# Two bidirectional mixers of a diffusion backbone: projections of the next group and head beside this one's work

## The reference, cut to what matters

```python
xbc = silu(short_conv(h @ w_in[x, B, C]) + conv_b)              # 3 taps; per group: 4 x tiles, B, C
lmat = exp(where(tril, acs[:, None] - acs[None, :], -inf))      # acs: cumulative dt * a, per head
y = (C B^T * lmat) @ (x dt) + (C @ state) * exp(acs)            # per chunk, forward and backward
state = state * exp(acs[-1]) + B^T @ (x dt exp(acs[-1] - acs))  # from chunk to chunk
out = rmsnorm((y_f + y_b + x * skip) * silu(z)) @ w_out         # SSD: 4 groups of 8 heads

q, k, v = silu(short_conv(h @ w_in)); q = l2norm(q) * dk ** -0.5; k = l2norm(k)
m = strict_tril((k beta) @ k^T * decay); tmat = inverse(I + m)  # 128 x 128 per chunk
v_new = tmat @ (v beta - (k beta exp(gc)) @ s)                  # chunk after chunk
o = (q exp(gc)) @ s + tril(q @ k^T * decay) @ v_new
s = s * exp(gc[-1]) + (k exp(gc[-1] - gc))^T @ v_new
out = (rmsnorm(o_f + o_b) * silu(z)) @ w_out                    # GDN: 8 heads, dk 128, dv 256
```

## Time and profile before

| | us |
|---|---|
| median of three runs (lowest, highest) | 6237.69 (6228.37, 6243.76) |
| the profiled execution: its own time, its span | 6234.22, 6232.4 |
| TensorE busy over the span | 4920.7 (79%) |
| VectorE busy | 4364.5 (70%) |
| ScalarE busy | 1670.4 (27%) |
| GpSimd busy | 1605.7 (26%) |

### The profile page before, as it was taken

How to read it: one execution, slowest core, us unless ns; L and a number is a source line. 1 busy time by engine, 2 the same in 40 slices (tenths; PEclk the granted TensorE clock), 3 DMA queues, 4 the chain that set the end, 5 groups by cost and what they waited for, 6 DMA issues and landing times. The chain is left out here.

```text
span 6232.4 us, 77006 instructions
## 1 busy us (share of the span) xinstructions
PE 4920.7 (79%) x27154; PEld 4314.5 (69%) x27154; DVE 4364.5 (70%) x7749; ACT 1670.4 (27%) x2016; POOL 1605.7 (26%) x1060
## 2 busy tenths in 40 slices
PE   6677676854689999997777777777854589999997
PEld 2566665754469888996766666666844359988896
DVE  1555554379759999998455555565279759999997
ACT  0122222211343333332212211121211243333332
POOL 0000000011026667773000000000011016666774
PEclk7788888877569999998888988899977559999999
DMA  8100110110159999995000000000110159999996
GB/s 359 40 28 21 38 38 4 54 38 23 71 234 402 401 401 397 397 398 209 29 25 25 25 25 21 16 18 21 54 38 23 54 217 401 401 402 398 397 395 261
DMA packets 340323, 1059.27 MB, mean 170 GB/s; under 512 B 28272, under 2 KB 135024, under 8 KB 316656
## 3 DMA queue, kind: packets, MB, share of 16 engines
q1 hardware_dynamic: 192624, 519.24, 22.0%
q0 software_dynamic: 147456, 536.94, 21.9%
HBM read 998.92 MB, written 57.15 MB: 169 GB/s over the span
## 5 line engine op out<-in xcount | busy, mean ns | idle before, releaser
L1836 POOL DMA_INDIRECT dense_ring<-in_peer_u_rows,dense_eid x512 | 723.3, 1413 | 934.6 <-DVEq L1952 583.8
L1608 POOL TENSOR_TENSOR top_w_lo<-top_w,top_w_hi 128x1024 fp32r<-128x1024 f32 x32 | 96.1, 3021 | 3342.4 <-ACTq L1576 3342.4
L1836 POOL DMA_INDIRECT dense_ring<-in_peer_v_rows,dense_eid x512 | 786.1, 1535 | 290.6 <-DVE dense_acc L1993 189.0
L1850 PE MATMUL psum<-peer_in_hi,dense_u_hi 128*128 128x384 f32 x2048 | 690.1, 337 | 44.8 <-DVE dense_u_lo L1958 44.8
L1850 PE MATMUL psum<-peer_in_hi,dense_u_lo 128*128 128x384 f32 x2048 | 690.4, 337 | 0.0
L1850 PE MATMUL psum<-peer_in_lo,dense_u_hi 128*128 128x384 f32 x2048 | 688.8, 336 | 0.0
L1993 DVE SCALAR_TENSOR_TENSOR dense_acc<-dense_ring,dense_weight,dense_acc 128x1024 f32<-128x1024 f32 x508 | 640.0, 1280 | 0.0
L1861 PE MATMUL psum<-dense_v_hi,dense_a_hi 128*128 128x512 f32 x1536 | 604.5, 394 | 18.7 <-DVE dense_a_lo L1972 17.1
L1985 DVE SCALAR_TENSOR_TENSOR dense_ring<-dense_ring,peer_rows 128x1024 f32<-128x1024 f32 x512 | 614.7, 1219 | 0.0
L1861 PE MATMUL psum<-dense_v_hi,dense_a_lo 128*128 128x512 f32 x1536 | 603.5, 393 | 0.0
L1861 PE MATMUL psum<-dense_v_lo,dense_a_hi 128*128 128x512 f32 x1536 | 602.8, 392 | 0.0
(11 more groups left out here) (339 smaller groups left out, 10170.4 us busy)
## 6 DMA issues: line engine op xcount, KB each, us to landing
dense_u<-in_peer_u SPq DMA_DIRECT2D x128, 1024.0 KB, 21.6
dense_v<-in_peer_v_rows SPq DMA_DIRECT2D x128, 1024.0 KB, 20.1
mod_w<-in_w_mod SPq DMA_DIRECT2D x24, 2048.0 KB, 16.7
gate_matrix<-gate_stage SPq DMA_DIRECT2D x12, 4096.0 KB, 11.1
dense_g<-gate_matrix SPq DMA_DIRECT2D x128, 384.0 KB, 15.6
gdn_w<-in_gdn_w_in SPq DMA_DIRECT2D x48, 512.0 KB, 3.4
ssd_w<-in_ssd_w_in SPq DMA_DIRECT2D x40, 512.0 KB, 3.3
top_w<-in_peer_w_q SPq DMA_DIRECT2D x32, 512.0 KB, 3.8
```

The costliest lines, as they stand in the source:

```text
L1608: nc.gpsimd.tensor_tensor(wlo[:, s].rearrange("p k n -> p (k n)"), w[:, s].rearrange("p k n -> p (k n)"), whi[:, s].rearrange("p k n -> p ...
L1836: nc.gpsimd.indirect_dma_start(ring[:, m % RING], None, table, bass.IndirectOffsetOnAxis(ap=eid[:, j, slot:slot + 1], axis=0)).then_inc(ro ...
L1850: last = nc.tensor.matmul(score_bank(e), w[:, e, cut], parts[x][:, kt, 0:DT], start=kt == 0 and n == 0, stop=kt == KT - 1 and n == 2)
```

## The change

Both loops over groups and heads are written out, so that each engine's order runs across their borders. A list `seq` gives the order of all projection tiles; while one group's or head's chain runs, the next one's tiles are projected. A projection now takes its two halves of 320 tokens one after the other, each in a PSUM bank of its own (three banks in SSD, two in GDN). ScalarE makes the high part of the weights and GpSimd the low part; `w` stays one buffer.

SSD: the masks of -1e30 are gone. One VectorE instruction makes the differences of both directions (1280 columns), one clamps them at zero, and C B^T is stored twice, multiplied by the triangle of each direction. `lm` has one buffer instead of two. GpSimd multiplies `ea` by C (for the 512 latent tokens only) and adds the two directions.

```diff
+def split_taps(nc, out, banks, w0, w2):
+    def add(shift, w):
+        for bank, base, lo, hi in ((0, 0, 0, BANKED), (1, BANKED, BANKED, LAT), (1, BANKED, LAT, T)):
+            a = lo + (shift < 0 and lo in STARTS)
+            b = hi - (shift > 0 and hi in ENDS)
+            to = out[:, a + shift:b + shift]
+            nc.vector.scalar_tensor_tensor(to, banks[bank][:, a - base:b - base], w, to, ALU.mult, ALU.add)
+    add(1, w0)
+    nc.vector.drain()
+    add(-1, w2)
...
+    def head_tiles(i):
+        following = [(i + 1, t) if i + 1 < SG else None for t in (XC, 0, 1, 2, 3)]
+        c, x0, x1, x2, x3 = following
+        return [c, (i, Z + 2), x0, (i, Z + 3), x1, None, x2, x3]
...
+            def increment(i, n):
+                c = incs[n][1]
+                pe.wait_ge(weighted, NI * i + n + 1)
+                if n == 0:
+                    pe.wait_ge(cb_ready, i + 1)
+                if n >= 2:
+                    pe.wait_ge(inc_used, NI * i + n - 1)
+                nc.tensor.matmul(inc_ps[n % 2], tok[:, c, SXT * P:], xw[n], start=True, stop=True).then_inc(inc_made, 1)
...
+                for n in range(4):
+                    increment(i, n)
+                if i + 1 < SG:
+                    project((i + 1, XB))
+                for n in range(4, NI):
+                    increment(i, n)
...
+                for r, tile in enumerate(head_tiles(i)):
+                    n = SR * i + r
...
+                    if tile is not None:
+                        project(tile)
+                    q, half = r // 2, (r % 2) * SP_
+                    if r % 2 == 0 and r:
+                        pe.wait_ge(heads_read, SXT * i + q)
+                    pe.wait_ge(ec_ready, n + 1)
...
+            def decay_row(i, r):
+                n = SR * i + r
+                act.wait_ge(sums_made, n + 1)
+                if n >= 2:
+                    act.wait_ge(m_used, n - 1)
+                nc.scalar.activation(ea[:, r % 2], sums_ps[:, :, 0:LAT], ACT.Exp).then_inc(ea_ready, 1)
+            def decay_matrix(i, r):
+                act.wait_ge(clamped, SR * i + r + 1)
+                nc.scalar.activation(lm[:], lm[:], ACT.Exp).then_inc(lm_exp, 1)
...
+                for r, tile in enumerate(head_tiles(i)):
+                    if r + 1 < SR:
+                        decay_row(i, r + 1)
+                    if tile is not None and at[tile] + 1 < len(seq):
+                        high(at[tile] + 1)
+                    if r + 1 < SR:
+                        decay_matrix(i, r + 1)
+                    if waiting is not None:
+                        silu(waiting)
+                        waiting = None
+                    if tile is not None and tile[1] >= Z:
+                        gate(tile)
+                    elif tile is not None:
+                        middle(tile)
+                        waiting = tile
...
+            def low(n):
+                pool.wait_ge(hi_ready, n + 1)
+                b = n % NW
+                nc.gpsimd.tensor_tensor(wlo[:, b].rearrange("p k n -> p (k n)"),
+                                        w[:].rearrange("p k n -> p (k n)"),
+                                        whi[:, b].rearrange("p k n -> p (k n)").bitcast(F32), ALU.subtract
+                                        ).then_inc(w_split, 1)
...
+            def times_c(i, r):
+                pool.wait_ge(ea_ready, SR * i + r + 1)
+                e = ea[:, r % 2]
+                nc.gpsimd.tensor_tensor(e, e, bcast(bc[:, i % 2, 1, 0:LAT], 1, [P, 2, LAT]), ALU.mult
+                                        ).then_inc(ec_ready, 1)
+            def add_directions(i, r):
+                n = SR * i + r
+                pool.wait_ge(lm_ready, n + 1)
+                if n >= 2:
+                    pool.wait_ge(m_used, n - 1)
+                if r < 2:
+                    pool.wait_ge(ctx_stored, 32 * (i + 1))
+                nc.gpsimd.tensor_tensor(m[:, r % 2], lm[:, FWD], lm[:, BWD], ALU.add).then_inc(m_ready, 1)
...
-            dve.sem_inc(w_split, 1)
-
-            def split_tile(i, t):
-                dve.wait_ge(w_loaded, 16 * (STILES * i + t + 1))
-                split_weights(nc, dve, whi[:, t % NW], wlo[:, t % NW], w[:]).then_inc(w_split, 1)
...
+            def difference(i, r):
+                n = SR * i + r
+                dve.wait_ge(ea_ready, n + 1)
+                if n:
+                    dve.wait_ge(m_ready, n)
+                nc.vector.tensor_tensor(lm[:].rearrange("p d (c j) -> p d c j", j=P),
+                                        sums_ps.rearrange("p d (c j) -> p d c j", j=P),
+                                        bcast(by_chunk(SACS, i, r), 3, [P, 2, NC, P]), ALU.subtract).then_inc(diff, 1)
+                dve.drain()
+                nc.vector.tensor_scalar(lm[:], lm[:], 0.0, None, ALU.min).then_inc(clamped, 1)
+            def weigh_matrix(i, r):
+                dve.wait_ge(lm_exp, SR * i + r + 1)
+                nc.vector.tensor_tensor(lm[:], lm[:], cb[:], ALU.mult)
+                dve.drain()
+                l4 = lm[:].rearrange("p d (c j) -> p d c j", j=P)
+                nc.vector.tensor_tensor(l4, l4, bcast(by_chunk(SDT, i, r), 3, [P, 2, NC, P]), ALU.mult
+                                        ).then_inc(lm_ready, 1)
```

```diff
+    units = [[(FWD, c) for c in range(NC - 1)], [(BWD, c) for c in range(NC - 1)], [(FWD, CTXC), (BWD, CTXC)]]
...
+    for i in range(GH):
+        if i + 1 < GH:
+            seq += [(i + 1, t) for t in range(GCONV)]
+        seq += [(i, Z), (i, Z + 1)]
...
+            def spread(key, values, half):
+                slots.claim(pe, key)
+                for n, c in enumerate(range(*CUT[half])):
+                    last = nc.tensor.matmul(side[slots.slot(key)][:, cs(n)], values[:, c:c + 1].to_broadcast([P, P]),
+                                            k.c("ident"), start=True, stop=True)
+                last.then_inc(slots.ready[slots.slot(key)], 1)
...
+            def level_product(i, n):
+                for u in range(NU):
+                    pe.wait_ge(level_ready[u], LEVELS * i + n + 1)
+                    pe.wait_ge(xt_ready[u], LEVELS * i + n)
+                    if n >= 2:
+                        pe.wait_ge(xi_ready[u], (NX - 1) * i + n - 1)
+                    for j, (dr, c) in enumerate(units[u]):
+                        last = nc.tensor.matmul(bank[u][:, cs(j)], level[:, dr, cs(c)], xt[:, dr, cs(c)],
+                                                start=True, stop=True)
+                    last.then_inc(lx_made[u], 1)
+                for u in range(NU):
+                    pe.wait_ge(lx_ready[u], NX * i + n)
+                    if n == 1:
+                        pe.wait_ge(xi0_ready[u], i + 1)
+                    for j, (dr, c) in enumerate(units[u]):
+                        last = nc.tensor.matmul(bank[3 + u][:, cs(j)], xi[:, dr, cs(c)], lx[:, dr, cs(c)],
+                                                start=True, stop=True)
+                    last.then_inc(xt_made[u], 1)
+                    if n < LEVELS - 1:
+                        for j, (dr, c) in enumerate(units[u]):
+                            last = nc.tensor.matmul(bank[u][:, cs(j)], lx[:, dr, cs(c)], xi[:, dr, cs(c)],
+                                                    start=True, stop=True)
+                        last.then_inc(xi_made[u], 1)
...
+                for n in range(1, LEVELS):
+                    level_product(i, n)
+                    if more and n == 1:
+                        squares(i + 1)
+                    if more and n == 2:
+                        project((i + 1, V))
+                    if more and n == 3:
+                        unit_rows(i + 1)
+                    if more and n == 4:
+                        project((i + 1, V + 1))
...
+                    fill = [3 * m + n for n in range(3)]
+                    for n, part in enumerate(("vn", "kv", "end")):
+                        if fill[n] < 2 * GVT * 3:
+                            at_fill = fill[n] * FILL
+                            tile = (i, Z + at_fill // (6 * KT))
+                            project(tile, at_fill % (6 * KT), at_fill % (6 * KT) + FILL)
...
+                for l in range(1, LEVELS):
+                    for u in range(NU):
+                        act.wait_ge(lx_made[u], NX * i + l)
+                        nc.scalar.copy(of_unit(lx, u), unit_ps(u, u)).then_inc(lx_ready[u], 1)
+                    if more and l == 2:
+                        roots(i + 1)
+                        high(n + 3)
+                    if more and l == 3:
+                        middle((i + 1, V))
+                        silu((i + 1, V))
+                        high(n + 4)
+                    if more and l == 5:
+                        middle((i + 1, V + 1))
+                        silu((i + 1, V + 1))
+                        high(n + 5)
...
+            def mask_level(i, n, u):
+                if n == 0:
+                    if i:
```

(114 more changed lines are left out.)

1251 lines of the change are left out of this document (682 added, 569 removed).

## The result

The changed kernel takes 5737.4 us (median of 4 runs, 5732.6 to 5740.2) against 6237.9 us (4 runs of before on the same chip): a ratio of 0.9198, 95% interval 0.9182 to 0.9214. The forecast was 5780 us, range 5640 to 5960. The profiled execution took 5740.2 us, its span is 5738.4 us.

The account below looks back on a forecast made before the run. No engine is full, so order was taken to bound both mixer stages. From 6234 us, 224 less in SSD (to 609) and 230 less in GDN (to 1162) give 5780 us, range 5640 to 5960.

Parts of the forecast that it names:

- Heads 87: SSD, a group's eight heads: 12.2 us each with a projection, some 11 without, 87 us in all.
- Last group 42 + 88: SSD's last group: 42 us and 88 us, the closing term of the stage's 583 us sum.
- The 26 us for the clock: SSD: 26 us added for stretches at 1.2 GHz, 5% of 504 us of work, giving 609 us.
- its 48: GDN's start: four first tiles and norms before the first head, 48 us.
- Inverse 67.5: GDN head's inverse with V's two projections, squares and unit rows, three stops left: 67.5 us.
- Scan 32: GDN head's scan: 26.0 us now; 96 filler matmuls add 14.1, lying in its gaps and beyond: 32 us.
- the 39 us: GDN: 39 us added for the clock, 4% of 980 us, on top of 1123, giving 1162 us.
- rival one: SSD: GpSimd and VectorE excluding each other costs 115 us in heads and 55 in openings, total 5950; chance 0.15.
- Rival two: GDN: in-order projections on TensorE delay awaited products, 20 of 28 us a head come back, total 5940; chance 0.10.
- Rival three: Both mixers: TensorE is full; with half of the forecast's waits gone, total 5650; chance 0.08.
- Rival four: SSD and GDN: GpSimd's unseen forms cost k times 2.28 ns an element; k 3.5 eats the gain, 4 gives 6380; chance 0.05.
- Rival five: Both mixers: some wait keeps projections out of the heads, only the reciprocals' 100 us is gained, 6130; chance 0.04.

Follow-up runs that it names:

- e12: Changed kernel with the next SSD group's six convolved tiles projected behind the group's heads instead of in its opening and heads: 5821.8 us.
- e3: Changed kernel with all of GpSimd's work in the SSD groups moved to VectorE: 5735.2 us.
- e8: Changed kernel with four GDN steps (transpose copies; K's taps, silu, squares; unit rows; V tiles' silu) reordered in their queues, no work added: 5657.2 us.
- e10: e8 plus, in each SSD group but the last, the third gate tile's projection moved from the second head into the opening: 5638.6 us.
- e7: Changed kernel with each GDN mask of levels one to six done twice on GpSimd: 5756.1 us.
- e4: Changed kernel with the next GDN head's four projections and all belonging to them put behind the head's outputs: 5830.6 us.
- e6: Changed kernel with the masks of levels two to six of the GDN inverse on VectorE instead of GpSimd: 5743.7 us.
- e5: Changed kernel with GDN's reciprocals taken over whole rows (1280 and 640 columns) instead of ten and five columns: 5832.0 us.
- e1: Changed kernel with its GDN heads as in the kernel before, SSD groups as changed: 5970.9 us.

## Why the prediction was right, step by step

**The total** was 43 us too high, 17 of it in SSD and 20 in GDN, by terms that partly cancel.

*SSD.* Start 51: 53.7. Opening 47: 46.3. Heads 87: 93.7. Here the step failed in its arithmetic: of eight decay sums one lies in the opening, and I took two off (2.2 us); a head with projection is 12.45, not 12.2, seven times; one starts at a low clock (1 us); TensorE waits 2.1 us. The 5.7 for the head without a projection should have been 2.2 + 2.9 = 5.1. Last group 42 + 88: 42.5 + 77.4. The chain is 9.6 us without the next group's tiles (e12), not 11: of the 3.0 us for handovers and for waiting on GpSimd beside the 8.05 of work, some 1.6 are left, by subtraction. The 26 us for the clock were laid on top of parts that came out with their slow stretches in them.

*GDN.* The start is the step that failed most: 48 forecast, 66 measured. The prediction does not show what its 48 is made of; I gave it SSD's weight cycle of 7.3 us, but the tiles came 10.4 us apart. GDN has two banks for projections where SSD has three, so each tile waits for the taps of the one before (9.4 us in three waits), and the norms wait for ScalarE's squares (5.4). Opening 30: 30.0 in the mean of heads two to seven. Inverse 67.5: 72.8; the three stops were named in advance, at 2, 5 and 4 us, and came as waits of 1.9 (behind K's taps rather than its silu), 2.9 and 3.0, with the low clock behind them and behind the squares, which I had put into a term of its own. Scan 32: 28.0, only 2 more than before without the 96 filler matmuls; they found more gaps than I gave them. Outputs 8.5: 8.1. Last head 109: 108.7. The period of a head, 138, came out at 138.1, by errors of 5 and 4 us that cancel: that agreement is luck. With 66 + 967 + 109 the stage needs no term for the clock: the 39 us were inside its parts.

**The exclusion** does happen, in SSD and in one place of GDN. Of the products with two SBUF inputs SSD's first rose to 2.23 us; GDN's one of 640 columns (L1811), 0.82 at least, took 1.62 in the median and up to 2.25, with GpSimd's split beside it, and GpSimd's masks wait for it. Subtractions with one operand in PSUM stayed at 0.69, and GpSimd's split went to 2.71 us in SSD and 2.39 in GDN. That is how the Trainium skill has it, "SBUF — State Buffer", section "Who interferes with whom": two inputs in SBUF contend with a GpSimd instruction that reads SBUF; one input, outside the two-port modes, does not. The clamp, one input, 826 to 1484 ns, fits the same section, which names `tensor_scalar` among the operations that can enter the two-port modes, and these contend too. But rival one priced it at 170 us in SSD and e3 at none: the mechanism was right, its place is off the path, because TensorE fills the heads. What it costs in GDN was not tried.

**Rival two** was half right, inside the forecast. TensorE's order did cost 12 us a head in the inverse, and e8 gets 80 us back; the projections hide the rest. **Rival three** (5650, TensorE full) is near where e10 ended, once the stops were gone. **Rival four**: GpSimd's unseen forms with two inputs cost 1.06 to 1.09 times the known 2.28 ns an element (1542 ns for 640, 1269 for 512), its per-partition scalars 1.6 and 2.1 times (923 ns for 256, 602 for 128), and e7 shows that even twice the price of the masks costs 19 us. Its sum for k = 3.5 was some 25 us too high: 10.15 less 6.7 is 3.45 us a level, not 3.9. **Rival five** fell with e4 and e12.

**Where the 500 us came from.** GDN's 251: overlap 93, compact reciprocals 95, and 63 left, which hold the three units, the weights' split off VectorE, GpSimd's masks (6 for five of seven levels, by e6, not told from none) and the jumps' 24. SSD's 242: overlap 84, GpSimd nothing, and 158 left for the compact chain (one difference of 1280 columns for ten, two products), the split's high part on ScalarE, and this loop's own jumps, at which VectorE sat idle for 9.8 us in three waits (L799). The windows place the 158 in the heads: a group's eight took 133.5 us before, with four gate tiles in them, and 76.6 in e12 with two. Two tiles are 14.2 us, and the other 42.7 a group are the heads' own chain; e3 leaves GpSimd out as their cause. Which part of the compact chain gave them, and how the 63 split, is by subtraction alone; none was undone by itself. What the prediction lacked is a price for the reciprocals in the new order. It gave them 100 us in the old one (rival five), and the views of VectorE, a third busy, suggest that they would be covered in the new; e5 shows that they would not.

## What to carry to other kernels

When work is interleaved into an engine's queue, set its price by the stretch with it less the stretch without it (31 us for 18.5 here), and look for the instructions of the next unit that stand ahead of the copies this one waits for: here each such stop also cost the slow clock behind it, and behind the squares it came without a stop. An engine that is a third busy can still hold the path, if what it is slow at sits in the banks that the next matmul writes. In SSD's heads work taken off VectorE, which does not set the pace, gained nothing by itself, and the contention that it brought cost nothing either: both are worth a run before they are worth an argument.

## What the runs showed of the hardware

At a loop's jump back VectorE sat idle for 4.3 us in the kernel before, and for 0.7 us at the same loop in e1, where only code ahead of it differed; in before an instruction queue brings 39 packets in the stage, one of them inside the 3.3 us wait shown above; in e1 it brings 4. The Trainium skill, "Runtime: NRT & Kernel Launch", section "Instruction fetch mechanics", says that a taken branch to a target outside the pages at hand waits for a fetch. The trace of before agrees with it, by its packets; that the idle time is this fetch is inferred from them, and why e1's loop is spared wasn't tried.
